# An encoder layer on eight cores: second FFN's output weights loaded in parts, and the first gates of a tile put ahead of the attention output's transposes

## What is computed

```
x = x + 0.5 * swiglu(rms_norm(x, ffn1_norm), ffn1_w_in, ffn1_w_out)      # width 2816
h = rms_norm(x, mix_norm); u, v, q, k, v_attn, g = split(h @ w_in)
a_out = u * (w_s @ rms_norm(v) + b)          # gelu before it, chunks of 128 tokens, 8 groups
b_out = rms_norm(diff_attention(q, k, v_attn, lam, rel_bias)) * (1 - lambda_init)
g_a, g_b = split(sigmoid(g + gate_bias))
x = x + (g_a * (a_out @ w_proj_a) + g_b * (b_out @ w_proj_b)) @ w_out
x = x + 0.5 * swiglu(rms_norm(x, ffn2_norm), ffn2_w_in, ffn2_w_out)
y = rms_norm(x, final_norm)
```

## Time and profile before

| | us |
|---|---|
| median of 3 runs (5548.26 to 5572.21) | 5553.7 |
| profiled execution: its own time | 5554.76 |
| its span on the slowest core, core 1 | 5553.2 |
| spans of the 8 cores | 5535.6 to 5553.2 |
| TensorE busy on core 1 | 5314.8 (96%) |
| mean granted clock, core 1 | 0.984 |

### The profile page before, as it was taken

How to read it: one execution, slowest core, us unless ns; L and a number is a source line. 1 busy time by engine, 2 the same in 40 slices (tenths; PEclk the granted TensorE clock), 3 DMA queues, 4 the chain that set the end, 5 groups by cost and what they waited for, 6 DMA issues and landing times.

```text
span 5553.2 us, 91906 instructions; the slowest of 8 cores (5535.6 to 5553.2 us)
## 1 busy us (share of the span) xinstructions
PE 5314.8 (96%) x34064; PEld 2653.9 (48%) x34064; DVE 1881.5 (34%) x3290; ACT 2412.9 (43%) x2966; POOL 512.0 (9%) x864
## 2 busy tenths in 40 slices
PE   6999999999988999999999999999979999999999
PEld 2444444444444445455555555555534444444444
DVE  3222222222275444554343343443232222222222
ACT  2222322221247555377777777777742122121211
POOL 1110101100031001410010000000000000000000
PEclk9999999999999999999999999999989999999999
DMA  9773536552310333212212222222172222232222
GB/s 187 164 154 115 138 118 151 144 141 91 118 69 35 124 118 113 77 71 88 102 66 94 88 74 100 72 84 94 66 199 108 105 104 106 99 111 106 103 80 76
DMA packets 198998, 590.33 MB, mean 106 GB/s; under 512 B 45568, under 2 KB 99456, under 8 KB 167328
## 3 DMA queue, kind: packets, MB, share of 16 engines
q1 hardware_dynamic: 114528, 536.16, 27.1%
q0 software_dynamic: 84032, 48.27, 7.3%
HBM read 531.99 MB, written 125.83 MB: 118 GB/s over the span
## 4 chain that ended last, share of the span: by engine, by line
PE 89%; ACT 3%; DVE 3%; issue 3%; DMA 2%; POOL 1%; DVEq 0%; SPq 0%; ACTq 0%; POOLq 0%
PE ps L716 33%; PE ps L765 16%; PE ps L1239 10%; PE ps L808 7%; PE ps L1210 7%; PE ps L1098 6%; PE ps L1139 3%; PE ps L1114 3%; PE ps L1220 3%; ACT arena L1227 2%; PE ps L582 1%; DMA arena<-xin 1%; DMA arena<-wscr 1%; PE ps L870 0%; DVE arena L1267 0%
## 5 line engine op out<-in xcount | busy, mean ns | idle before, releaser
L716 PE MATMUL ps<-arena 128*128 128x512 bf16 x8448 | 1864.4, 383 | 20.9 <-DVE arena L721 10.2
L1227 ACT ACTIVATE arena<-ps,arena 128x1024 bf16<-128x1024 f32 x1280 | 1367.6, 1117 | 434.6 <-PE ps L1210 231.3
L716 PEld LDWEIGHTS ps<-arena 128*128 128x128 bf16 x8448 | 828.3, 99 | 1015.4 <-issue 86.8
L765 PE MATMUL ps<-arena 128*128 128x512 bf16 x4224 | 920.4, 379 | 0.0
L721 DVE TENSOR_TENSOR arena<-ps,arena 128x512 bf16<-128x512 f32 x528 | 364.9, 691 | 1401.2 <-PE ps L716 1075.9
L1239 PE MATMUL ps<-arena 128*128 128x129 bf16 x10240 | 814.8, 222 | 9.7 <-DVE arena L1245 6.7
L719 ACT ACTIVATE arena<-ps 128x512 f32<-128x512 f32 x528 | 312.9, 594 | 1096.7 <-PE ps L716 1084.9
L1239 PEld LDWEIGHTS ps<-arena 128*128 128x128 bf16 x10240 | 612.1, 98 | 244.0 <-issue 228.9
L765 PEld LDWEIGHTS ps<-arena 128*128 128x128 bf16 x4224 | 412.0, 98 | 490.5 <-issue 2.8
L553 ACT ACTIVATE arena<-arena 128x1024 bf16<-128x1024 f32 x192 | 202.8, 1056 | 951.2 <-DVE arena L552 922.2
L1210 PE MATMUL ps<-arena 64*128 64x512 bf16 x2560 | 505.4, 389 | 62.6 <-ACT arena L1227 51.6
(11 more groups left out here) (94 smaller groups left out, 3070.5 us busy)
## 6 DMA issues: line engine op xcount, KB each, us to landing
arena<-wscr SPq DMA_DIRECT2D x185, 1024.0 KB, 5.0
arena<-wscr SPq DMA_DIRECT2D x96, 768.0 KB, 4.4
arena<-xin SPq DMA_DIRECT2D x96, 512.0 KB, 6.4
arena<-x2d SPq DMA_DIRECT2D x96, 512.0 KB, 5.6
arena<-hTd SPq DMA_DIRECT2D x36, 1024.0 KB, 5.3
x1d<-arena SPq DMA_DIRECT2D x48, 512.0 KB, 2.6
arena<-x1d SPq DMA_DIRECT2D x48, 512.0 KB, 5.5
x2d<-arena SPq DMA_DIRECT2D x48, 512.0 KB, 2.9
```

Of the source, the lines that this page charges most:

```text
L716: A("pe", lambda e, k=k, w=w, col=col, bank=bank, c=c, t=t: e.matmul(out=psbank(bank), lhsT=w[:, k, col:col + 128], rhs=xnT[c % 2][:, k, t ...
L765: A("pe", lambda e, s=s, j=j, half=half, bank=bank: e.matmul(out=psbank(bank), lhsT=act_of(s)[:, j * 128:(j + 1) * 128], rhs=wout[:, s, ha ...
L1227: A("act", lambda e: e.activation(out=PT[slot], in_=PS[pi][:, :], func=AF.Exp, bias=bt[:, h:h + 1]), reads=[("ps", 2 * pi), ("ps", 2 * pi ...
```

## The change

Three things are changed. The two loads of the second FFN's output weights leave `second_begin`; eleven loads of one eleventh each take their place in the first chunk of FFN 2, one at every third step. In `post_tasks` the gates and the first branch of a tile no longer come after the transposes; only the second branch of column block 0 waits for the last of them. In the stretch at the mixer's end the transposes get a lag of 9 us on the builder's clock (task `ended`), and the ring of PSUM banks is cut to banks 4 to 7.

```diff
@@ second_begin
                 rings[0] = Ring(range(2), pieces, fill)
-                wout_load(0, 6)
-                wout_load(6, 5)
                 come = Task(0.0, lambda: None, [])
@@ body
                         if u % 4 == 3:
                             rings[0].release(buf)
+                        if second and c == 0 and u % 3 == 0 and u // 3 < 11:
+                            wout_load(u // 3, 1)
@@ post_tasks
                     tk = Task(0.25, lambda j=j: bo(j), last)
                     tasks.append(tk)
                     last = [(tk, 1.5)]
-                last = last + list(end)
+                last_bo = last[0][0]
+                last = list(end)
                 for oc in range(8):
                     for f, w in ((gate, 1.73), (branch, 0.87)):
                         for which in range(2):
                             tk = Task(w, lambda oc=oc, which=which, f=f: f(oc, which), last)
+                            if (f, oc, which) == (branch, 0, 1):
+                                tk.deps = tk.deps + [(last_bo, None)]
@@ mix_stage
             attention(4, 8, uv)
-            run_tasks(([] if record else f2_begin()) + post_tasks(11, [], []), clock)
+            banks[0] = [4, 5, 6, 7]
+            ended = Task(0.0, lambda: None, [])
+            run_tasks([ended] + ([] if record else f2_begin()) + post_tasks(11, [(ended, 9.0)], []), clock)
```

## The result

The ratio of the changed kernel to the kernel before is 0.9957, with a 95% interval of 0.9944 to 0.9969: 0.43% faster, within half a per cent, as forecast. On the 5553.7 us shown ahead that is 5529.8 us, against a forecast of 5532. The undisturbed executions of the changed kernel took 5528.79, 5530.54, 5533.15 and 5534.59 us, those of the kernel before beside them 5548.26 to 5572.21. All rows of after are from core 1.

The account below looks back on a forecast made before the run. TensorE, busy 96% of the span, was taken as the bound. Gains of 15 us in the stretch, 1.2 at FFN 2's start and 5.8 in tiles 3 and 11 made 22: 5532 us against 5553.7, range 5516 to 5550.

Parts of the forecast that it names:

- I take 3.5 us: Stretch at the mixer's end: loss to TensorE's lower clock, 11 us before, would be 3.5 us (0 to 11).
- Part 1, the loads: Output weights leave the stretch for FFN 2's first chunk: three waits for weight pieces, 10.5 us, gone.
- I charge 1 us: Stretch: first two of eleven parts, issued about when the last two `wo` pieces are requested, cost 1 us (0 to 4).
- The cover in the first chunk: FFN 2's first chunk: its own matmuls hide the parts' loading at no cost; without it 17.5 us at worst.
- Part 2, the order at the mixer's end: Gates ahead of transposes: 3.6 of 7.86 us wait for `obn` left, new wait of 1.0 us for `boT` copies.
- Part 3, the banks: Four-bank ring in the stretch: 3.98 us wait at FFN 2's first matmul gone, 13.8 us of new waits (3 to 24).
- eaten gain: Rival: ScalarE, DMA and clock at upper costs; 1 us won in the stretch, 4 in tiles; 5549 us, chance 0.13.
- Part 4, tiles 3 and 11: Gates fill the waits for `obn` in tiles 3 and 11: 5.0 us of waits and 0.8 of clock, 5.8 (2 to 8).
- four banks cost little: Rival: stretch waits 3 to 6 us for 13.8, clock near 1, stretch 71 us; 5517 us, chance 0.27.
- the ring in series: Rival: each of 8 blocks waits 5.9 us for its predecessor's bank, 47 us for 13.8; 5565 us, chance 0.03.
- The clock at its lower level throughout: Rival: lower clock from first `bo` to block 7, TensorE's 34 us become 68; 5554 to 5561 us, chance 0.04.
- No part landed late: Rival: a weight part lands late, so the first L765 waits up to 17.5 us; 5550 us, chance 0.03.

Follow-up runs that it names:

- e2: Kernel before with only the output weights' loads moved into FFN 2's first chunk, old order and eight banks; stretch 86.5 us, undisturbed execution 5538.8 us.
- e5: Changed kernel with the eleven weight parts issued at steps 6 to 36 instead of 0 to 30; stretch 81.5 us, undisturbed executions 5529.8 to 5536.6 us.
- e9: Changed kernel itself, timed again beside the kernel before; ratio 0.995 (0.9913 to 0.9987), undisturbed executions 5528.0 to 5538.8 us.
- e4: Changed kernel with a ring of banks 2 to 5 in place of 4 to 7; stretch 76.5 us, undisturbed execution 5523.2 us.
- e3: Changed kernel with the ring of all eight banks kept in the last stretch; ratio 0.9968 (0.9953 to 0.9983), stretch 84.7 us.
- e7: Changed kernel with e5's later parts, six banks without 6 and 7, two more gates and one branch ahead of the transposes; stretch 65.5 us, executions 5511.3 to 5535.1.
- e6: Changed kernel with e4's banks 2 to 5 and e5's later parts together; stretch 71.6 us, undisturbed executions 5531.5 and 5553.8 us.
- e8: Changed kernel with the old order in every tile but the last stretch; stretch 85.0 us, no undisturbed execution time.
- e10: Kernel of e7 unchanged, timed again in more rounds beside the kernel before; executions 5520.55 and 5525.47 us, 0.65% faster by the medians.
- e1: Changed kernel with the two big output-weight loads back in second_begin; stretch 93.3 us, undisturbed execution 5538.2 us.

## Where the prediction was right, and the step that failed

The forecast was 22 us by three steps, against 21.0 in the parts: 15 in the stretch (13.3 measured over the cores, 12.2 on core 1), 1.2 at FFN 2's start (2.4), 5.8 in tiles 3 and 11 (5.3 to 9.3). The waits that it foresaw are there, and the total is right; but inside the stretch and inside the tiles errors cancel, and that is luck. The step that failed is the clock's, "I take 3.5 us": it cost about 9. On core 1:

| term | forecast | measured |
|---|---|---|
| wait for bank 5 | 1.15 | 1.46 |
| rest of the wait for `obn` | 3.6 | 3.25 |
| new wait for the copies of `boT` | 1.0 | 1.00 |
| waits behind banks and ScalarE | 13.8 | 9.4 |
| lower clock (and all else) | 3.5 | 9.0 |
| second `wo` piece | 1 | 2.9 |
| with 60.2 of work | 84.3 | 87.2 |

**Part 1, the loads.** Right in mechanism: e2 shows that they alone carry the region's gain. The step "I charge 1 us" for the two parts that meet the second `wo` piece was mis-sized: the collision is real (e5) and cost 2.0 to 4.0 us of wait (1.1 to 3.6 in e9) and about as much again in clock. By the prediction's own list ("no wait for wscr", "if pieces are still late") this is a sign of being wrong. The cover in the first chunk held. The parts of 512 KB took 19.4% of 152 us for 4.72 MB, 6.2 us of all engines per MB, the big loads 38.4 us for 5.77 MB, 6.7 per MB. So no price for small parts shows; but the DMA share around them was 0.55 and around the big loads 0.88, so that size was not the only difference. The Trainium skill's "DMA: Bandwidth & Descriptors", "Rules for kernel authors", would have transfers of 1 MiB or more; this trace does not show a loss below it, and the measurement decides:

```profile
q0 software_dynamic: 2448, 4.72, 19.4%
...
arena<-ffn_w_out POOLq DMA_DIRECT2D x9, 512.0 KB, 6.3
```

**Part 2, the order at the mixer's end.** Right to 0.35 us in both waits.

**Part 3, the banks.** The meeting of `nb` with the ring was found where it was forecast: blocks 1, 2 and 7 show 1.48 us each for 1.6, and block 4 shows 3.16 for 3.7. Block 3 shows 1.05 for 1.1. The 1.4 at block 0 and the 1.0 behind block 4 didn't come. The sum was 4.4 us too large, mostly because lower clock, charged elsewhere, gave ScalarE time to keep up. That last reason is argued, not shown.

**The clock** is the term that was mis-sized most: 3.5 us, where 9.0 were left over (8, with the same 1 us for overlap that the prediction took off its 12.2 of before). It was to shrink from 11 with the idle pieces, and it hardly shrank. Two things in the traces say why. First, some 3 us of the 11 were no lower level: core 1 of before spent 16 us of its stretch at the steady 0.81 shown above, which is neither of the two levels nor a mean of them. On cores 4 to 7, which had none of it, 7.2 us were left over before; the changed kernel has 8.1 and, in e9, 6.9. Next to nothing came back. Second, the lower level costs only while TensorE works. Behind the wait of 7.86 us the kernel before spent ten microseconds at 0.50, but stood still for over half of them:

```profile
4063.00:4073.00 10.00, 4.72 (x21) 0.50 0.95 265
```

In the changed kernel the windows from 4055 and from 4089 us hold 5.00 and 5.34 us of work at 0.50. Half of such work is loss: some 2.4 us behind the one long wait, 2.5 and 2.7 behind each of two shorter ones. The prediction had such a price at hand: it named 16 matmuls that took 5.40 us for 3.46, and its rival of the eaten gain says that a wait of 3.7 us may lower the clock. Against 3.5 for the clock and 1 for the `wo` piece (9.0 and 2.9 measured) stand 13.8 for the banks (9.4): 7.4 us too little and 4.4 too much.

**Part 4, tiles 3 and 11.** The step came out in size, by two errors. Waits of 5.0 us were to go, and 3.4 went: 2.09 us for `obn` stay in tile 11, and tile 3 has a new wait of 1.75 us for the copies that the forecast had only for the last stretch. Of the lower clock, priced at 2.7 us, 0.8 was to come back, and the windows show 1.00.

**The rivals.** That the four banks cost little is refuted (e4: without the sharing the stretch is 10 us shorter), and so is the ring in series. The clock at its lower level throughout is refuted too, with 0.90 over the stretch. The eaten gain didn't come, but its reason did: the wait of 3.16 us in the middle lowered the clock. The rule of the Trainium skill named beside it ("TensorE: Matmul & The Clock Gate", "A second HAM failure mode: psum-queue depth-cycling") is borne out in part: a wait made by the bank ring lowered the clock, but it was the one of 3.16 us; around those of 1.48 the windows show 1.00. No part landed late. The forecast that the cut to four banks gains 3.98 us was half of the truth: e3 shows that what it won at FFN 2's first matmul it lost behind the block transposes.

## What to carry to other kernels

Price a lower clock by the work that TensorE does in it, not by the length of the wait that came first: one wait of 7.86 us cost no more clock here than one of 3.16. So a long wait that is split into several of about 3 us gains less than it seems. From the changed kernel to e7, whose longest wait is 1.8 us, 13.3 us of idle time were removed and 7.7 us of lower clock went with them, while e2 had 21.7 us of idle time and lost only 4.6 to the clock. When a ring of PSUM banks is given to the work between two stages, take out the banks that something else uses outside the ring before counting how many are left; which four mattered by 10 us, but four or eight, both with the shared banks 6 and 7, by nothing. And a large load that is moved away from a tight place still has a first part: put that, too, behind the last tight request.

## What was not expected of the hardware

From e5 on some cores, always in neighbouring pairs, ran the mixer's first 200 us with some 140 us at a steady granted clock of 0.81 while others of the same execution had 1.00 for most of them: cores 2 and 3 of e5, 0 to 3, 6 and 7 of e6, 2 to 7 of e7, 0, 1, 6 and 7 of e8, 0 and 1 of e9, 0 to 3 of e10. They took 2564 to 2573 us for the mixer where their neighbours took 2541 to 2558. The same window on core 0 and then on core 3 of e5:

```profile
1520.00:1600.00 80.00, 67.54 (x406) 0.95 0.29 106
```

```profile
1520.00:1600.00 80.00, 78.83 (x389) 0.81 0.25 93
```

The kernels' code is the same there. It shifts a core's span by some 17 us, nearly as much as the whole change. The profiles of e1 to e4 don't have it on their undisturbed cores, nor has the changed kernel's; cores 0 to 3 of before have the same 0.81 in shorter pieces elsewhere, above all in FFN 1. What sets it off stays open; it was not tried.
